# A hybrid decode step: K pages three per tile, the decode softmax two tiles earlier, twelve V pages beside the last four projection tiles

## The reference, cut to what matters

```python
def diff_attend(q, k, v, qpos, kpos, lam):
    s = jnp.einsum('bqhcd,bkhcd->bhcqk', q, k).astype(jnp.float32)
    p = masked_softmax(s, kpos[None, :] <= qpos[:, None])
    a = p[:, :, 0] - lam * p[:, :, 1]
    return jnp.einsum('bhqk,bkhv->bqhv', a.astype(v.dtype), v)
...
    k_all = jnp.concatenate([gather(cache_dk), k_d], axis=1)
    v_all = jnp.concatenate([gather(cache_dv), v_d], axis=1)
    o_d = diff_attend(q_d, k_all, v_all, pos, jnp.arange(past + T), lam)
```

## Time and profile before

| | |
|---|---|
| median of three runs | 878.2 us |
| the profiled execution's own time | 880.67 us |
| its span | 878.8 us (1.87 us lie outside it) |
| granted PE clock over the span | 0.937 of full |
| PE busy | 792.2 us, 90% |
| DVE busy | 451.8 us, 51% |
| ACT busy | 189.3 us, 22% |
| bytes moved | 221.62 MB, 252 GB/s over the span |
| stage two, tiles 0 to 15 | 313.7 to 508.33 us |
| four V steps and the window products | 508.33 to 523.03 us |
| stage three, rounds | 523.03 to 807.7 us |

### The profile page before, as it was taken

How to read it: one execution, slowest core, us unless ns; L and a number is a source line. 1 busy time by engine, 2 the same in 40 slices (tenths; PEclk the granted TensorE clock), 3 DMA queues, 4 the chain that set the end, 5 groups by cost and what they waited for, 6 DMA issues and landing times.

```text
span 878.8 us, 14940 instructions
## 1 busy us (share of the span) xinstructions
PE 792.2 (90%) x4891; PEld 381.3 (43%) x4891; DVE 451.8 (51%) x980; ACT 189.3 (22%) x484; POOL 19.7 (2%) x38
## 2 busy tenths in 40 slices
PE   6999999899988799999999998897888867887998
PEld 2555544355343434454535662342433323335443
DVE  2133234354305438678536357575775673584923
ACT  1310020001002002122224213242342341243000
POOL 0000000000000100010001010000000000000000
PEclk9999999999999989999999978898978897997999
DMA  9987697969979697978683179995788888682011
GB/s 343 319 260 220 243 364 252 378 222 335 338 248 352 217 354 265 352 259 331 224 265 128 37 249 307 333 307 186 229 281 271 269 266 293 221 353 120 1 48 50
DMA packets 136873, 221.62 MB, mean 252 GB/s; under 512 B 17482, under 2 KB 65779, under 8 KB 135323
## 3 DMA queue, kind: packets, MB, share of 16 engines
q1 hardware_dynamic: 113930, 197.40, 65.3%
q10 hardware_dynamic: 20528, 14.27, 5.3%
q0 software_dynamic: 2336, 8.99, 3.1%
HBM read 214.72 MB, written 10.04 MB: 256 GB/s over the span
## 4 chain that ended last, share of the span: by engine, by line
PE 62%; SPq 14%; DVE 11%; DMA 9%; issue 4%; ACT 0%; ACTq 0%; DVEq 0%
PE banks L591 13%; PE banks L613 13%; SPq L383 9%; PE banks L1031 6%; PE banks L627 4%; PE banks L844 4%; PE banks L559 3%; DMA proj<-in_cmp_cache 3%; DVE att L1714 2%; PE banks L874 2%; DMA ring<-in_dv_cache 2%; DMA ring<-in_dk_cache 2%; PE banks L912 2%; PE banks L890 2%; SPq L378 2%
## 5 line engine op out<-in xcount | busy, mean ns | idle before, releaser
L613 PE MATMUL banks<-ring,xt 128*128 128x512 f32 x448 | 199.7, 599 | 0.0
L613 PEld LDWEIGHTS banks<-ring,xt 128*128 128x128 f32 x448 | 83.4, 191 | 104.7 <-issue 104.6
L1261 ACT ACTIVATE wide<-banks,att 128x128 f32<-128x128 f32 (+3 forms) x128 | 66.3, 523 | 179.8 <-DVE att L1714 174.3
L591 PE MATMUL banks<-proj,wide 128*64 128x256 f32 x896 | 102.2, 390 | 1.7 <-DMA proj<-in_cmp_cache 1.7
L844 PE MATMUL banks<-ring,small 128*32 128x512 f32 x512 | 80.0, 705 | 20.7 <-DMA ring<-in_dv_cache 17.9
L591 PEld LDWEIGHTS banks<-proj,wide 128*64 128x64 f32 x896 | 65.2, 141 | 40.9 <-DMA proj<-in_cmp_cache 7.0
L627 PE MATMUL banks<-ring,small 128*32 128x512 f32 x512 | 62.8, 612 | 16.9 <-DMA ring<-in_dk_cache 16.9
L1439 DVE TENSOR_SCALAR small<-small 128x510 f32<-128x510 f32 x8 | 3.4, 426 | 143.5 <-ACT small L1100 128.6
L1085 ACT ACTIVATE proj<-banks,x_rs 128x512 f32<-128x512 f32 x32 | 22.0, 687 | 216.4 <-PE banks L613 207.1
L890 PE MATMUL banks<-consts,wide 128*128 128x128 f32 x240 | 45.4, 317 | 16.9 <-DVE xt L1738 8.8
L874 PE MATMUL banks<-proj 32*128 32x128 f32 (+7 forms) x256 | 59.6, 546 | 0.0
(11 more groups left out here) (342 smaller groups left out, 812.4 us busy)
## 6 DMA issues: line engine op xcount, KB each, us to landing
ring<-in_dk_cache SPq DMA_DIRECT2D x256, 256.0 KB, 5.9
ring<-in_dv_cache SPq DMA_DIRECT2D x256, 256.0 KB, 4.0
proj<-in_cmp_cache SPq DMA_DIRECT2D x144, 128.0 KB, 3.9
ring<-in_w_in SPq DMA_DIRECT2D x7, 2048.0 KB, 10.0
proj<-in_cmp_cache ACTq DMA_DIRECT2D x80, 128.0 KB, 5.6
ring<-in_x_nat SPq DMA_DIRECT2D x2, 2048.0 KB
ring<-in_cmp_cache SPq DMA_DIRECT2D x32, 128.0 KB, 3.8
ring<-in_w_out SPq DMA_DIRECT2D x1, 4096.0 KB, 12.4
```

The lines of the kernel that those rows point to most:

```text
L591: last = mm(to, w1[:, kv, half, lp, :], rows[:, kv, g, lp, :, :, :], start=lp + half == 0, stop=lp == LP - 1 and half == 1, tile_position= ...
L613: last = mm(banks[:, 3 + n % 2, :], xt[:, k, P * t:P * t + P], w_ring[:, c % 2, k, :], start=k == 0, stop=k == KC - 1)
L1261: last = A(e_slot(j, c)[:, 0:n], banks[:, 2 * (j % 2) + c, 0:n], ACT.Exp, bias=row_max[:, j % 4, c:c + 1], accum_out=row_sum[:, j % 4, c:c ...
```

## The change

- `K_LATE` is 3 for every tile, so the K steps end behind tile 9 instead of tile 11.
- The softmax of the decode scores moves up: DVE takes the maximum behind `silu_z(25)`, ACT takes the exponential in tile 10, DVE computes the weights behind `silu_z(26)`, and the 32 turning products stand behind tile 11. Their result goes into every other 512 columns of the score row itself (`wide`) instead of `small8`, and the prompt's probability slots (`e_slot`) take the other halves of `wide` and `small8`.
- Twelve V steps (`V_EARLY` = 12) stand behind tiles 12 to 15 (3, 3, 2, 4). The first pick stands behind tile 15. The 52 others are spread over rounds 0 to 58 by `v_round`; the rounds 7, 14, 22, 29, 37, 44, 52 and 59 have none.
- The compressed branch of the prompt uses banks 5 and 6 instead of 6 and 7, and its DVE part stands behind `silu_z(27)`, `sum_new(7)`, the window weights and the gates instead of in front of them.
- The loads: the weights of chunk 7 come behind all K pages. Of the first half's 104 blocks SP issues 26 between the loads of V pages 4 to 11, ACT 26 and the first two fixed rows in tiles 13 to 15 and 26 in rounds 0 to 18, SP the last 26 beside the V loads 15 to 27. Of the second half SP issues its 52 behind the V loads 36 to 57. `sel_run` reads up to four block numbers at a time.

```diff
-        K_STEPS, K_TURN, K_LATE = 64, 6, (3, 2, 2)
-        V_EARLY = 4
+        K_STEPS, K_TURN, K_LATE = 64, 6, 3
+        V_EARLY, V_ROUNDS = 12, 60
...
+        def v_round(v):
+
+            return (v - V_EARLY) * V_ROUNDS // (K_STEPS - V_EARLY)
+
+        def pick_round(b):
+
+            return v_round(8 * b + 8) if b < DEC - 1 else V_ROUNDS
...
+        def sel_run(eng, kind, n, end):
+
+            while n < end:
+                q, slot = n // N_TOP, SEL_FIRST + n % N_TOP
+                to = min(end - n, N_TOP - n % N_TOP, 4)
+                sel_ranked(eng, kind, q, slot, slot + to)
+                n += to
...
             for v in range(64):
+                load_v(v)
                 if v == 4:
                     sp.wait_ge(s("proj_ready"), 28)
                     sp.wait_ge(s("new_proj_ready"), 7)
-                    for b in range(2):
-                        sel_fixed(sp, mybir.EngineType.SP, b)
-                    for q in range(4):
-                        sel_load(q)
-                if v == 8:
+                if 4 <= v < 11:
+                    sel_run(sp, mybir.EngineType.SP, 26 * (v - 4) // 7, 26 * (v - 3) // 7)
+                if v == 15:
                     sp.wait_ge(s("proj_ready"), 32)
                     sp.wait_ge(s("new_proj_ready"), NCHUNK)
-                if 8 <= v < 21:
-                    sel_ranked(sp, mybir.EngineType.SP, 7, v - 6, v - 5)
-                if v == 32:
+                if 15 <= v < 28:
+                    sel_run(sp, mybir.EngineType.SP, 78 + 2 * (v - 15), 80 + 2 * (v - 15))
+                if v == 36:
                     sp.wait_ge(s("sel_tensor"), sel_step(0, "sel_valued"))
...
+                if 36 <= v < 58:
+                    sel_run(sp, mybir.EngineType.SP, 156 + 52 * (v - 36) // 22, 156 + 52 * (v - 35) // 22)
...
                 if i == 11:
...
+                    pe.wait_ge(s("scores_kept"), 8)
+                    pe.wait_ge(s("diff_weights"), 1)
+                    for g in range(PAGES):
...
                 if i == 12:
-                    pe.wait_ge(s("scores_kept"), 8)
+                    pe.wait_ge(s("probs_kept"), 4)
+                    for v in range(3):
+                        v_step(v)
+                    pe.wait_ge(s("new_proj_used"), 8)
...
+                    for v in range(3, 6):
+                        v_step(v)
...
+                    v_step(6)
+                    v_step(7)
+                if i == 15:
                     pe.wait_ge(s("c_turned_kept"), 2)
...
+                    pick(0)
                     turn_blocks("z6")
                     turn_blocks("z7")
+                    for v in range(8, V_EARLY):
+                        v_step(v)
...
-                if j < DUOS and j % 8 == V_EARLY:
-                    pick(j // 8)
-                if j + V_EARLY < 64:
-                    v_step(j + V_EARLY)
+                for b in range(1, DEC):
+                    if j == pick_round(b):
+                        pick(b)
+                for v in range(V_EARLY, 64):
+                    if j == v_round(v):
+                        v_step(v)
...
+                if i == 10:
+                    act.wait_ge(s("diff_max"), 1)
+                    A(scores, scores, ACT.Exp, bias=work[:, 144:145], accum_out=work[:, 145:146]).then_inc(s("diff_exps"), 1)
...
+                    for b in range(2):
+                        sel_fixed(act, mybir.EngineType.Activation, b)
+                    sel_run(act, mybir.EngineType.Activation, 26, 30)
...
+                    sel_run(act, mybir.EngineType.Activation, 30, 39)
...
+                    sel_run(act, mybir.EngineType.Activation, 39, 52)
```

More of the change, by code:

```diff
@@ L347, in late_k @@
         def late_k(i):
-            before = K_TURN * 6 + sum(K_LATE[n % 3] for n in range(min(i, 12)))
-            return range(before, before + (K_LATE[i % 3] if i < 12 else 0))
+            before = K_TURN * 6 + K_LATE * i
+            return range(before, min(before + K_LATE, K_STEPS))
+        def v_round(v):
+            return (v - V_EARLY) * V_ROUNDS // (K_STEPS - V_EARLY)
+        def pick_round(b):
+            return v_round(8 * b + 8) if b < DEC - 1 else V_ROUNDS
         def duo(j):
@@ L689, in _, with v_step, pick @@
                     k_step(n)
+            def v_step(v):
+                b, st = v // 8, v % 8
+                pe.wait_ge(s(f"page_in{st % 4}"), 64 * (K_STEPS // 4 + 2 * b + st // 4 + 1))
+                if st == 0 and b > 0:
+                    pe.wait_ge(s("o_diff_kept"), b)
+                for i in range(4):
+                    last = mm(banks[32 * i:32 * i + 32, 7, :], probs_t[:, st // 2, 4 * (st % 2) + i, 32 * (b // 4):32 * (b // 4) + 32],
+                              k_ring[:, st % 4, i, :], start=st == 0, stop=st == 7, tile_position=(0, 32 * i))
+                last.then_inc(s("v_used"), 1)
+            def pick(b):
+                pe.wait_ge(s("v_masked"), b + 1)
+                for m in range(4):
+                    last = mm(banks[:, 7, m:m + 1], v_masked(b)[:, m // 2, P * (m % 2):P * (m % 2) + P], ones[:, 0:1],
+                              start=True, stop=True)
+                last.then_inc(s("v_picked"), 1)
             for i in range(16):
@@ L919, in values @@
                 last.then_inc(s("pv_n"), 1)
-            def pick(b):
-                pe.wait_ge(s("v_masked"), b + 1)
-                for m in range(4):
-                    last = mm(banks[:, 7, m:m + 1], v_masked[:, m // 2, P * (m % 2):P * (m % 2) + P], ones[:, 0:1],
-                              start=True, stop=True)
-                last.then_inc(s("v_picked"), 1)
             def sel_scores(n):
@@ L1217, in _ @@
                     A(gates, gates, ACT.Exp, scale=-1.0).then_inc(s("gate_exps"), 1)
+                    for h in range(4):
+                        act.wait_ge(s("probs_turned"), h + 1)
+                        A(wide[:, 1024 * h:1024 * h + 512], banks[:, 6 + h % 2, :], ACT.Copy).then_inc(s("probs_kept"), 1)
                 if i == 12:
@@ L1235, in _ @@
                     keep_turn("z5")
-                    for h in range(4):
-                        act.wait_ge(s("probs_turned"), h + 1)
-                        A(probs_t[:, 8 * h:8 * h + 8, :].rearrange("p g n -> p (g n)"), banks[:, 6 + h % 2, :], ACT.Copy).then_inc(s("probs_kept"), 1)
                     act.wait_ge(s("new_proj_used"), 7)
@@ L1625, in _ @@
             silu_z(25)
+            keep_scores(7)
+            dve.wait_ge(s("scores_kept"), 8)
+            V.tensor_reduce(work[:, 144:145], scores, AX.X, ALU.max, negate=True).then_inc(s("diff_max"), 1)
             dve.wait_ge(s("p_kc_roots"), 1)
@@ new lines, in _ @@
+            dve.wait_ge(s("diff_exps"), 1)
+            L(V.reciprocal(work[:, 145:146], work[:, 145:146]))
+            L(V.tensor_tensor(small[:, 58:59], small[:, 58:59], work[:, 145:146], ALU.mult))
+            V.tensor_scalar(own_rows, const("bmap"), scores[:, PAST:PAST + 1], None, ALU.mult)
+            V.tensor_scalar(own_weights, const("hmap"), small[:, 58:59], None, ALU.mult)
+            V.tensor_scalar(d_weights, const("dmap"), small[:, 58:59], None, ALU.mult).then_inc(s("diff_weights"), 1)
@@ L1636, in _ @@
-            keep_scores(7)
-            dve.wait_ge(s("scores_kept"), 8)
-            V.tensor_reduce(work[:, 144:145], scores, AX.X, ALU.max, negate=True).then_inc(s("diff_max"), 1)
-            dve.wait_ge(s("c_scored"), 1)
-            by_tile = banks[:, 6:8, :].rearrange("p g (t r n) -> p g t r n", t=TILES, r=GRP)
-            for g in range(2):
-                last = V.tensor_tensor(by_tile[:, g, :, :, :], by_tile[:, g, :, :, :],
-                                       bc(const("cmpneg").rearrange("p (t n) -> p t n", t=TILES), GRP, 2), ALU.add)
```

159 lines of the change are left out of this document (64 added, 95 removed).

## The result

The changed kernel takes 884.4 us (median of 20 executions, 875.93 to 889.29) beside 878.6 us for the kernel before on the same chip (20 executions, 873.11 to 885.76). The ratio is 1.006, its 95% interval 1.0034 to 1.0085: slower by 0.6%, where 870.3 us was forecast. Ratios leave out executions more than 1.5% above the fastest of their kernel (one of the 20 of the changed kernel); the medians keep them.

The account below looks back on a forecast made before the run. PE was taken to bound the tiles, while the rounds lost 52 us of PE time, with SP's issue rate making pages late. Tiles +13.0 and rounds -20.9 gave -7.9: 870.3 us, own range 862 to 876, terms' ends 858 to 881.

Parts of the forecast that it names:

- Page 11 is then 4.5 us late: Behind tile 15: PE waits for V page 11, +4.5 us (0 to 7), and lower clock after it, +0.5.
- SP's count: V step 0 to page 11's issue: 26 blocks (22.4 us) and seven and a bit page loads (20 to 22), 42.5 us.
- the three holes: PE's idle gaps at the compressed branch and hand-over in tiles 13 and 14, filled by other work: -1.8 us (worst 0).
- The K steps: Three K steps per tile in tiles 0 to 9, with a tighter supply of pages: +1.5 us (0 to 6).
- The moved softmax: Weights must be ready before the products behind tile 11; cover 3.5 us, costed at nothing, up to 3 us if gone.
- the two terms: Fewer late V pages: rounds 7 to 10, -3.5 us (0 to -4.6); rounds 39 to 49, -6.5 (-2 to -13).
- rounds 20 and 52: Waits behind DVE's late selected blocks in these rounds shrink: -3 us (-1 to -5).
- The carry to the median: Execution's own time 872.8 us, less the 2.5 us between it and the median, gives 870.3 us.
- D: Tiles: `diff_weights` or a K page comes late beyond the cover; +9 us on top of the forecast, 879; chance 0.09.
- A: Rounds are a chain of DVE and ACT, so the tiles' +13 us is not repaid: +10, 888; chance 0.12.
- B: Page 11 on time and late pages vanish entirely: tiles +8.5 or less, rounds -32, 854 us; chance 0.18.
- C: The wait only moves, since SP issues as many DMAs: rounds -13 us, no change, 878; chance 0.13.

Follow-up runs that it names:

- the kernel with K alone: Kernel before with only the new K steps (three behind each of tiles 0 to 9) and loads of weights: 879.8 us, ratio 1.000 to before.
- the kernel with the later store: Changed kernel with GpSimd's 1 MB store of `p_dv` waiting until V step 11 is over: 882.8 us, ratio 1.006 to the kernel before.
- the last experiment: Changed kernel with V steps 10 and 11 moved behind the 64 window products on PE: 878.2 us, ratio 0.9985 to the kernel before.

## Why the prediction was wrong, step by step

**The step that failed is "Page 11 is then 4.5 us late, with nothing on PE behind it but the window products: +4.5 (0 to 7). PE may come out of that wait at the lower clock: +0.5."** The mechanism was right in the main, and the kernel with the blocks taken off SP shows it; the size was not. It measured 9.97 us of waiting, plus 1.9 for two V steps at half the rate, plus 2.6 for the window products (13.82 against 11.20): 14.5 us in place of 5.0. Page 11 came 11.0 us after PE, undelayed, would have needed it (515.6), not 4.5. Page 10 was late too, which the sum did not have; since page 11 was later still, that adds no waiting, but it brought the lower clock one V step sooner. Three things were short:

- SP's count. From the end of V step 0 (474.8) to the issue of page 11 (520.77) it was 45.9 us, not 42.5; the register read of 3.64 us, of a kind whose median is 0.47, is as large as the difference. The sum had also taken the lower end of its own terms: 22.4 and 20 to 22 us make 42.4 to 44.4.
- The page's own loads. PE could start on page 11 5.9 us after its first issue (526.63 - 520.77), where 3 was taken. The landing of 3.73 us is in the range that the sum gave (2.5 to 4.3); the other 2.1 us are the issue of the page's four loads, one of which took 0.85 us instead of 0.33.
- The clock. I gave it 0.5 us. Behind a wait of 5.18 us PE stayed at the 1.2 GHz level for all of the next 22 us. The earlier trace rows had shown the same (0.52 behind a wait of 3.97), and I used them in the rounds only. By the kernels without the waits (products of 9.45 to 11.61 us, in one 12.61) the clock is worth 2.2 to 4.4 us in the products alone (1.2 by that one).

The Trainium skill (DMA: Bandwidth & Descriptors, "Issuing engines are not separate DMA queues") calls the time of issue usually small beside the DMA itself. The trace disagrees here, as the prediction had it: with 26 small blocks between seven pages on SP, PE waited 10.0 us for two pages, and with these blocks taken off SP it waited for none of them.

**The other terms of the tiles** held. The pick took 1.05 us. Two of the three holes went, the one of 0.39 us at line 1142 stayed (-1.4 for -1.8). The K steps waited once, 0.90 us, for 1.5, and the kernel with K alone gave a ratio of 1.000. The moved softmax cost nothing: the products began at 457.81 with no wait. With eight V steps at 0.92 us (7.4) all terms together make 22.4 us, and the tiles grew by 20.5. Most of the 1.9 between is that the kernel before lost some 1.7 us near 396 us at a lower clock, where a tile took 8.28 us and the changed kernel's 7.03; no term had this.

**The rounds** were 263.9 us for 263.8, with errors that cancelled. Late pages fell by 11.5 us for the 10.0 of the two terms; rounds 20 and 52 gave 3.5 for 3; waits for DVE grew by 5.1, where half of 8.5 had been kept for this. What I had not counted is ACT: the waits for its copies (line 1284) grew by 5.4 us. PE's busy time fell by 14.3 us, of which V steps and pick are 9.6 and the rest, 4.8, is clock (0.87 for 0.86) for the 2 expected.

**The carry to the median** was the second error, as large as the first. The tiles' error and the start of the first tile make the execution 6.3 us longer than forecast (879.1 against 872.8); the other 7.8 of the 14.1 us are that I took 2.5 off for the median and should have added 5.3. The median granted clock is 0.932 for the kernel before (in the experiments) and 0.926 after, and in the slowest execution of the kernel with the later store the rounds alone took 11 us more of PE at 0.82 than at 0.87. So by these numbers the change bought less waiting in the rounds and paid with a lower clock; the second trace of the changed kernel (881.9 us, 2.1 of its 2.8 us more in the rounds) points at the rounds too, but no trace of this kernel reaches its median of 884.4. Eight V steps early remove the waits in the tiles and raise the clock to 0.947. That order of clocks follows the order of times in nearly all of the kernels in the table, but order is not cause: what makes PE lose its clock in the rounds of one execution and not of the next was not isolated and stays open. So does what the twelve early steps would be worth with no wait and no drop of the clock at all.

**The rivals of the prediction.** D (the K pages or the softmax late) is out: one wait of 0.90 us. A (a chain of DVE and ACT keeps the rounds long) is out: they shrank by 20.8 us. B needed page 11 on time. By their times A (888) is nearest to the median and D (879) and C (878) to the trace, which is luck in A and D. In C, "the wait only moves", the rounds were to shrink by 13 us and shrank by 20.8; the last experiment shows that it is nonetheless in part how the pages behave: late pages grew by 8.2 us in the rounds where 10.0 us of waits went ahead of them, though the rounds grew by 2.0 only. The advice of the Trainium skill (Perfetto Trace Analysis, "Optimization Strategy" under "Identifying Performance Opportunities") that interleaving regimes with different limits may pay held with eight V steps (0.985 and 0.983) and not with twelve (1.006).

## What to carry to other kernels

Before work is moved to where an engine is full, count the issues of the queue that feeds it from one step to the next, the late item's own among them, add a landing time from a stretch that is as loaded as this one will be, and leave out the steps whose data the sum has late: two V steps fewer turned +0.6% into -1.1%, and four into -1.5 to -1.7%. Price a wait of several microseconds with the clock behind it; here that was 4.5 us on top of 10. And compare a kernel's clock over many executions before a few microseconds are carried from one trace to a median.

## What the runs showed of the hardware

- A register read on SP that has a median of 0.47 us took 3.64 and 3.63 us in two traces, each time when GpSimd's store was issued 1.6 us ahead of it. With the store later the longest was 1.37; with the store in its old place but another time between it and SP's reads the longest was 0.68 to 1.63 in nine traces.
- The same 64 window products took 9.45 us at a granted clock of 0.76, 10.56 to 10.76 at 0.65 or 0.66, 11.20 to 11.61 at 0.61 to 0.63, 12.61 at 0.55 and 13.82 at 0.50; 13.82 came after each wait of 4.5 us or more. The clock was below full in them in all fourteen traces, also in the kernel before, where PE had no wait ahead of them.
- A V step took 1.06 us behind a wait of 3.96 us, 1.50 behind one of 4.50 and 1.93 or 1.94 behind waits of 4.51 to 5.35.
- The last load of a page landed 3.7 us behind its issue for page 11 of the changed kernel, 6.2 us for page 10 beside the store, and 7.3 us for page 11 with nine blocks on ACT. One page load held SP's queue for 0.85 and 1.27 us in the two traces of the changed kernel; the median is 0.33.
- The clock also fell where PE had at most a short wait before. A tile near 400 us took 7.5 to 9.1 us instead of 7.03 in twelve of fourteen traces. In the changed kernel it took 7.03, with a wait of 0.90 us a little ahead of it; in the kernel before it took 8.28 with none. One near 484 us took 9.7 to 9.9 us in three traces, with PE busy without a gap for more than 80 us ahead of it.
